# Loading the past values later in seven pairs of heads and earlier in the last

## The chip, the cores and the metric

The kernel runs on one core of a Trainium2 chip. The metric is the time of one execution in device microseconds (us); a run is the median of several executions, and one further execution is profiled. The engines are TensorE (PE), VectorE (DVE), ScalarE (ACT), GpSimd (POOL) and SyncE (SP), which here does nothing but issue transfers.

## The reference, cut to what matters

One layer of a decoder: 512 new tokens of one sequence, and one token for each of 8 sequences with a stored past of 2048 keys and values. Rows of 520 tokens are multiplied with one input projection, and the part that the change touches is the attention of the 8 single tokens over their past.

```
h = rms_norm(x);  u, gp, q, k, v, ga = split(h @ w_in)        # 2048 -> 6 x 1024, 16 heads of 64
for each of the 8 sequences and each head:                    # the sampled tokens
    positions = last 128 one by one, last 512 every 4th, last 2048 every 16th, and the token itself
    s = q . k[positions] - slope * distance;  p = softmax(s) per pattern, patterns combined
    a = sum(p * v[positions])
x = x + concat(pool_branch * silu(gp), a * silu(ga)) @ w_out;  y = rms_norm(x)
```

## The kernel before

The work is written out by hand. A **pair** is two of the 16 heads with 128 of the pool channels; there are 8 pairs (`pr` 0 to 7). A pair has 18 **chunks** (`j` 0 to 17): six column tiles of the projection, each in three chunks of 5 or 6 blocks of 128 rows. All five engines walk through the same list of steps, one chunk a step, each in its own order of instructions, and meet only at semaphores. After the 144 chunks of the input projection come 48 of the output projection. A pair's later work (`j` 18 to 25) is done in the first steps of the next pair.

A chunk of weights goes this way: SP loads it into one of three slots of `w_raw` (L442, 320 or 384 KB, three steps ahead of its use), ACT makes the rounded high part `w_hi` (L864), DVE the remainder `w_lo` (L1217), and PE multiplies (L660). SP may issue chunk n+3 only when DVE has finished chunk n, so SP runs about two steps ahead of PE. The scores, probabilities and transposes of the prompt's attention stand between a chunk's matmuls in PE's own order: in the last pair `turn_p(7, 0, 1)` (transposes, L704, in step 11) needs the normalised probabilities from ACT (L916, which needs DVE's reciprocal L1302), and `turn_p(7, 0, 2)` in step 12 also needs DVE's `p_lo(7, 0, 1)` (L1308).

The past of the 8 sequences comes in three loads of keys (`load_keys`, in steps 5, 6 and 7) and three of values (`load_values`, L469), of 512, 384 and 384 KB, all from SP's queue. The token's own row of q, k and v is spread over partitions by four small transfers each (`spread_rows`, L481, in steps 6, 8 and 12). Once the k row has landed, POOL writes it out (`send_k_row`, L1160, 4 KB), and the third part of DVE's `keys` (L1332), which multiplies in place, waits for that write:

```
def keys(pr, t):
    ...
    dve.wait_ge(k_in, 48 * pr + 48)
    dve.wait_ge(row_in[0], 16 * SQS * (pr + 1))
    if t == 2:
        dve.wait_ge(row_in[1], 16 * SQS * (pr + 1))
        dve.wait_ge(kn_st, 16 * pr + 16)
```

The steps in which DVE does `keys` and `values` are in the plan: `kq=(17, 18, 19)` and `vm=(20, 21, 21)` for the first seven pairs (USUAL), `kq=(8, 9, 10)` and `vm=(13, 14, 14)` for the last (FINAL). `values` waits for all three loads of values and for the exponentials.

Of the kernel before, what the change touches and what calls it, by code (L numbers as in the profile page):

```python
# [62 lines left out]


class Plan:
    def __init__(self, qk, s, kn, ur, kq, ex, ns, pt, vm, vr, av, pick, mix, gate):
        self.qk, self.s, self.kn, self.ur = qk, s, kn, ur
        self.kq, self.ns, self.pt, self.vm, self.vr, self.av = kq, ns, pt, vm, vr, av
        self.ex = ex
        self.pick, self.mix, self.gate = pick, mix, gate  # L70


USUAL = Plan(qk=(7, 12), s=(8, 13), kn=13, ur=15, kq=(17, 18, 19), ex=20, ns=20, pt=22,
             vm=(20, 21, 21), vr=(22, 23), av=24, pick=25, mix=(19, 21), gate=20)
FINAL = Plan(qk=(7, 11), s=(8, 12), kn=20, ur=19, kq=(8, 9, 10), ex=12, ns=17, pt=19,
             vm=(13, 14, 14), vr=(18, 20), av=20, pick=21, mix=(17, 18), gate=19)
PLANS = (USUAL,) * (PAIRS - 1) + (FINAL,)

# [42 lines left out]
def layer_step(nc, x_prompt, x_sample, state_pool, cache_k, cache_v, norm_g, w_in, pool_w,  # L121
               pool_scale, w_out, final_g, consts, y_prompt, y_sample, pool_state_p, k_win_p,
               v_win_p, pool_state_s, k_new, v_new):
    with ExitStack() as ctx:
# [110 lines left out]
        av = take(P)  # L235
# [128 lines left out]
        def due(step):  # L364

            pr, j = divmod(step, NCH)
            if pr > PAIRS:
                return ()
            late = ((pr - 1, j + NCH, PLANS[pr - 1]),) if pr > 0 else ()
            return late + (((pr, j, PLANS[pr]),) if pr < PAIRS else ())  # L370

        def chunk_of(n):

            if n < IN_CHUNKS:
                return divmod(n % NCH, 3)
            return OUT_SEQ[n - IN_CHUNKS]
# [55 lines left out]
        def _(sp):  # L432

            def load_chunk(n):
                t, c = chunk_of(n)
                lo, hi = span_of(n)
                dst = w_raw[:, n % SLOTS, 0:hi - lo, :]
                if n >= SLOTS:
                    sp.wait_ge(w_lo_done, n - 2)
                if n < IN_CHUNKS:  # L440
                    at = COL_OF[t] + P * (n // NCH)
                    sp.dma_start(dst, wi[:, lo:hi, at:at + P]).then_inc(raw_in[n % SLOTS], 16)  # L442
                    return
                cols = slice(P * t, P * t + P)
                if n >= TAIL and c > 0:
                    for at, k, m in (((0, 8, 5), (5, 6, 1)), ((0, 7, 1), (1, 13, 3)))[c - 1]:
                        sp.dma_start(dst[:, at:at + m, :],
                                     wo[:, k:k + m, cols]).then_inc(raw_in[n % SLOTS], 16)
                elif c == 2:
                    sp.dma_start(dst[:, 0:2, :], wo[:, 6:8, cols]).then_inc(raw_in[n % SLOTS], 16)  # L450
                    sp.dma_start(dst[:, 2:5, :], wo[:, 13:16, cols]).then_inc(raw_in[n % SLOTS], 16)
                else:
                    at = OUT_K[lo]
                    sp.dma_start(dst, wo[:, at:at + hi - lo, cols]).then_inc(raw_in[n % SLOTS], 16)
# [10 lines left out]
            def load_past(dst, rows, pr, t, done):  # L465

                lo = POS_AT[t][0]
                to = dst[:, P * lo:P * (lo + POS_T[t])].rearrange("p (s x) -> p s x", x=P)
                sp.dma_start(to, rows[t][:, :, P * pr:P * pr + P]).then_inc(done, 16)  # L469

            def spread_rows(pr, i):

                new_pos = slice(P * (POS - 1), P * POS)
                to = (q_rep, kk[:, new_pos], vv[:, new_pos])[i]
                sp.wait_ge(row_turned[i], pr + 1)
                if pr > 0 and i < 2:
                    sp.wait_ge(kq_sum, 3 * pr)
                elif pr > 0:
                    sp.wait_ge(av_done, pr)
                for a in range(SQS):  # L480
                    sp.dma_start(to[:, SQ * a:SQ * a + SQ],  # L481
                                 row_sq[i][SQ * a:SQ * a + NB, :].unsqueeze(1).to_broadcast(
                                     [NB, PARTS, SQ])).then_inc(row_in[i], 16)

            def load_keys(pr, t):
                if t == 0 and pr > 0:
                    sp.wait_ge(kq_sum, 3 * pr)
                load_past(kk, k_rows, pr, t, k_in)

            def load_values(pr, t):  # L490
                if t == 0 and pr > 0:
                    sp.wait_ge(av_done, pr)
                load_past(vv, v_rows, pr, t, v_in)

            def reload(i):
                k = OUT_K[i]
                r = RELOADED.index(i)
                if r == 0:
                    sp.wait_ge(pmix_st, 16 * len(RELOADED))
                    sp.wait_ge(kq_sum, 3 * PAIRS)  # L500
                sp.dma_start(mix_in[r], mix_dram[k]).then_inc(mix_back[r], 16)
# [18 lines left out]
            for step in range(IN_CHUNKS + OUT_CHUNKS):  # L520
                if step + 3 < IN_CHUNKS + OUT_CHUNKS:
                    load_chunk(step + 3)
                for pr, j, p in due(step):
                    if j == 8:
                        sp.dma_start(st_nat[0:NB * HIST, :],
                                     st[:, P * pr:P * pr + P]).then_inc(st_in, 16)
                    if j == 0:
                        if pr % 2 == 1:
                            sp.dma_start(pw_raw, pw[pr // 2:pr // 2 + 1].rearrange(
                                "a p c d -> (a p) c d")).then_inc(pw_in, 16)  # L530
                    if j in (5, 6, 7):
                        load_keys(pr, j - 5)
                    if j in (10, 11, 12):
                        load_values(pr, j - 10)
                    if j in (6, 8, 12):
                        spread_rows(pr, (6, 8, 12).index(j))
                    if j == 14:
                        sp.wait_ge(v_nat_c, pr + 1)
                        sp.dma_start(v_out[:, :, P * pr:P * pr + P],
                                     v_nat.rearrange("p (t x) -> p t x", t=QT)).then_inc(kv_st, 16)  # L540
                    if j == p.kn + 3:
                        sp.wait_ge(k_turned, pr + 1)
                        for a in range(SQS):
                            at = P * pr + SQ * a
                            sp.dma_start(k_sq_out[:, :, at:at + SQ],
                                         k_sq[SQ * a:SQ * a + SQ, :].rearrange(
                                             "p (c x) -> p c x", x=SQ)).then_inc(kv_st, 16)
                n = step - IN_CHUNKS
                if n == -4:
                    for r in range(3):  # L550
                        reload(RELOADED[r])
                for i in {-1: (3, 4, 5), 0: (6, 7, 8), 1: (9, 10), 2: (13, 14)}.get(n, ()):
                    load_split(i)
                if n == 7:
                    sp.wait_ge(m_split, len(SPLIT_ORDER))
                    sp.wait_ge(kv_st, KV_ST * PAIRS)
                    for e in range(3):
                        load_res(e)
                if n >= 0:
                    d, c = chunk_of(step)  # L560
                    if c == 0 and d >= 4:
                        sp.wait_ge(y_scaled, d - 3)
                        load_res(d - 1)
# [290 lines left out]
        def _(act):  # L854
# [82 lines left out]
            def early(pr, j, p):  # L937
# [9 lines left out]
                if j == p.qk[0]:  # L947
                    qk_hi(pr, 0)
                if j == p.qk[1] and p is USUAL:
                    qk_hi(pr, 1)  # L950
# [25 lines left out]
            def late(pr, j, p):  # L976
# [20 lines left out]
                if s1 + 1 <= j < s1 + 4:  # L997
                    exps(pr, 1, j - s1 - 1)
                if j == p.qk[1] and p is FINAL:
                    qk_hi(pr, 1)  # L1000
# [197 lines left out]
        def _(dve):  # L1198
# [289 lines left out]
            def early(pr, j, p):  # L1488
                n = NCH * pr
                s0, s1 = p.s  # L1490
                if s0 + 2 <= j < s0 + 5 and not (p is FINAL and j == p.qk[1] + 1):
                    turn_den(pr, 0, j - s0 - 2)
# [12 lines left out]
                if j == 12:  # L1505
                    if p is FINAL:
                        p_lo(pr, 0, j - s0 - 3)
# [16 lines left out]
                if j == p.pick:  # L1524
                    pick_heads(pr)
                if s0 + 3 <= j < s0 + 6 and not (p is FINAL and j == 12):
                    p_lo(pr, 0, j - s0 - 3)
# [4 lines left out]
                if s1 + 1 <= j < s1 + 4:  # L1532
                    bias_unit(pr, 1, j - s1 - 1)
                if j == 17 and p is FINAL:
                    split_pooled(pr)
# [293 lines left out]
```

## Time and profile before

| | |
|---|---|
| median of 3 runs | 850.28 us (850.09 to 852.3) |
| the profiled execution | 850.75 us, of it 848.9 from the first to the last instruction (the span) |
| PE busy | 838.7 us, 99% of the span, 6895 instructions |
| DVE busy | 555.2 us, 65% |
| ACT busy | 383.0 us, 45% |
| transfers issued by SP and others on queue 1 | 115.44 MB, 50.5% of 16 engines' span |

The profiled execution is longer than its span by 1.85 us, which lie outside of the instructions. A busy PE says that matmuls are under way, not that they run at their peak; whether an engine is waited for is read from the waits and the chain.

### The profile page before, as it was taken

To read this page: it belongs to the slowest core of one execution; us is meant where nothing else is said; L and a number is where in the kernel's file an instruction comes from. 1 tells how busy PE (TensorE), PEld (TensorE's weight loads), DVE (VectorE), ACT (ScalarE), POOL (GpSimd) and SP (SyncE) were. 2 spreads that over 40 slices of the span, in tenths; PEclk is the share of its full clock that TensorE was granted. 3 is DMA by queue.
4 is the path that set the end of the run, shared out by engine and by line. 5 is a ranking of instruction groups with operands and counts; after the bars stand their busy time and mean duration, and the time that the engine had idled before them with its cause. 6 is when DMAs were issued, how large, how long until landed. Compare 5 with 4: busy or idle time off the path is not lost.

```text
span 848.9 us, 17355 instructions
## 1 busy us (share of the span) xinstructions
PE 838.7 (99%) x6895; PEld 833.5 (98%) x6895; DVE 555.2 (65%) x1198; ACT 383.0 (45%) x849; POOL 60.7 (7%) x116
## 2 busy tenths in 40 slices
PE   9999999999999999999999999999999999999995
PEld 8999999999999999999999999999999999999995
DVE  4647784797579577857885796679888443333445
ACT  4745435523553464245435524553464354333433
POOL 2100100201010001002000101010001000000000
PEclk9999999999999999999999999999999999999999
DMA  8576347536643763574366337634759534434435
GB/s 287 144 171 163 88 127 180 132 97 176 158 110 95 192 149 86 151 186 120 97 166 172 100 100 204 156 94 129 191 164 313 145 112 116 116 106 123 120 109 202
DMA packets 236520, 124.04 MB, mean 146 GB/s; under 512 B 38256, under 2 KB 230080, under 8 KB 236416
## 3 DMA queue, kind: packets, MB, share of 16 engines
q1 hardware_dynamic: 231832, 115.44, 50.5%
q0 software_dynamic: 4608, 7.50, 2.6%
q8 instruction: 55, 0.90, 0.5%
q14 instruction: 25, 0.20, 0.1%
HBM read 106.59 MB, written 15.20 MB: 143 GB/s over the span
## 4 chain that ended last, share of the span: by engine, by line
PE 98%; DVE 1%; ACT 1%; issue 0%; DVEq 0%
PE pj L660 83%; PE ps_t L704 3%; PE pj L686 1%; PE ps_o L748 1%; PE ps_s L719 1%; PE ps_s L717 1%; PE ps_o L746 1%; PE ps_t L765 1%; PE ps_s L765 1%; PE ps_o L660 1%; PE ps_s L660 1%; PE ps_m L704 1%; PE ps_s L601 1%; PE pj L621 0%; PE pj L697 0%; PE ps_o L612 0%
## 5 line engine op out<-in xcount | busy, mean ns | idle before, releaser
L660 PE MATMUL pj<-mov_hi,w_hi 128*128 128x260 f32 x1952 | 400.8, 287 | 0.3 <-DVE mov_lo L1238 0.3
L660 PE MATMUL pj<-mov_hi,w_lo 128*128 128x260 f32 x1952 | 393.3, 283 | 0.0
L660 PE MATMUL pj<-mov_lo,w_hi 128*128 128x260 f32 x1952 | 392.5, 283 | 0.0
L660 PEld LDWEIGHTS pj<-mov_hi,w_hi 128*128 128x128 f32 x1952 | 300.9, 189 | 1.0 <-issue 0.6
L660 PEld LDWEIGHTS pj<-mov_lo,w_hi 128*128 128x128 f32 x1952 | 301.0, 189 | 0.0
L660 PEld LDWEIGHTS pj<-mov_hi,w_lo 128*128 128x128 f32 x1952 | 301.0, 189 | 0.0
L1217 DVE TENSOR_TENSOR w_lo<-w_raw,w_hi 128x640 fp32r<-128x640 f32 (+1 forms) x187 | 161.8, 865 | 157.2 <-ACT w_hi L864 156.8
L864 ACT ACTIVATE w_hi<-w_raw 128x640 fp32r<-128x640 f32 (+1 forms) x187 | 144.5, 773 | 230.2 <-PE pj L660 213.9
L924 ACT ACTIVATE pt_hi<-ps_t 128x128 fp32r<-128x128 f32 (+1 forms) x64 | 26.3, 436 | 82.4 <-PE ps_t L704 79.5
L1308 DVE TENSOR_TENSOR pt_lo<-ps_t,pt_hi 128x128 fp32r<-128x128 f32 (+1 forms) x64 | 29.7, 485 | 45.0 <-ACT pt_hi L924 44.8
L1255 DVE SCALAR_TENSOR_TENSOR arena<-pj,rstd_bc 128x260 f32<-128x260 f32 (+2 forms) x104 | 36.9, 399 | 12.1 <-PE pj L660 10.3
L908 ACT ACTIVATE arena<-arena,stat 128x128 f32<-128x128 f32 (+1 forms) x64 | 35.8, 560 | 18.5 <-DVE stat L1294 17.9
L1294 DVE CUSTOM_DVE_ANT_0 arena<-ps_s,arena 128x128 f32<-128x128 f32 (+1 forms) x64 | 29.7, 482 | 16.9 <-PE ps_s L719 16.9
L916 ACT ACTIVATE arena<-arena,stat 128x128 f32<-128x128 f32 (+1 forms) x64 | 34.2, 558 | 12.2 <-DVE stat L1302 12.0
L1063 ACT ACTIVATE arena<-arena 128x128 f32<-128x128 f32 (+1 forms) x70 | 21.8, 311 | 28.9 <-DVE arena L1662 27.2
L704 PE MATMUL ps_t<-tab,arena 128*128 128x128 f32 x218 | 34.0, 272 | 0.0
L1368 DVE TENSOR_TENSOR arena<-arena 128x128 f32<-128x128 f32 (+3 forms) x48 | 28.8, 601 | 1.6
L704 PEld LDWEIGHTS ps_t<-tab,arena 128*128 128x128 f32 x218 | 26.2, 141 | 2.1
L1335 DVE TENSOR_REDUCE arena<-arena 128x16 f32<-128x1024 f32 (+2 forms) x24 | 26.1, 1086 | 0.8
L1332 DVE TENSOR_TENSOR arena<-arena 128x1024 f32<-128x1024 f32 (+2 forms) x24 | 26.0, 1083 | 0.0
L1359 DVE TENSOR_TENSOR arena<-arena 128x1024 f32<-128x1024 f32 (+2 forms) x24 | 25.4, 1087 | 0.2
L1176 POOL DMA_DIRECT2D out<-arena x32 | 16.3, 510 | 104.7 <-DVE arena L1607 104.7
(243 smaller groups left out, 812.4 us busy)
## 6 DMA issues: line engine op xcount, KB each, us to landing
w_raw<-in_w_in SPq DMA_DIRECT2D x96, 320.0 KB, 3.5
w_raw<-in_w_in SPq DMA_DIRECT2D x48, 384.0 KB, 3.7
arena<-in_cache_k_win SPq DMA_DIRECT2D x16, 384.0 KB
arena<-in_cache_v_win SPq DMA_DIRECT2D x16, 384.0 KB
w_raw<-in_w_out SPq DMA_DIRECT2D x16, 384.0 KB, 3.5
w_raw<-in_w_out SPq DMA_DIRECT2D x16, 320.0 KB, 3.2
arena<-in_cache_k_win SPq DMA_DIRECT2D x8, 512.0 KB
arena<-in_cache_v_win SPq DMA_DIRECT2D x8, 512.0 KB
```

The source lines that it names most:

```text
L660: mm = pe.matmul(dst[h][:, 0:HT], w, m[:, k, HT * h:HT * h + HT], start=(k == 0 and i == 0), stop=(c == 2 and k == KT - 1 and i == 2))
L704: return pe.transpose(dst, src, ident[0:n, 0:n])
L864: act.activation(w_at(n)[0][:, 0:hi - lo, :], w_raw[:, n % SLOTS, 0:hi - lo, :], ACT.Copy).then_inc(w_hi_done, 1)
L908: act.activation(pb_, pb_, ACT.Exp, scale=-1.0, bias=nmax[:, i:i + 1], accum_out=den[:, i:i + 1]).then_inc(exped, 1)
L916: a = act.activation(pb_, pb_, ACT.Copy, scale=rden[:, i:i + 1])
L924: a = act.activation(pt_hi[:, 0:i + 1, P * i:P * i + P], ps_t[:, at:at + P * (i + 1)].rearrange("p (j x) -> p j x", j=i + 1), ACT.Copy)
L1217: dve.tensor_tensor(to_lo[:, 0:hi - lo, :], w_raw[:, n % SLOTS, 0:hi - lo, :], to_hi[:, 0:hi - lo, :].bitcast(F32), ALU.subtract).then_inc ...
L1255: o = dve.scalar_tensor_tensor(out=dst, in0=pj[a][h][:, c0:c1], scalar=scale, in1=rstd_bc[:, HT * h + c0:HT * h + c1], op0=ALU.mult, op1=A ...
L1294: dve.tensor_tensor_reduce(out=pbuf[r % 2][:, at:at + n], in0=ps_s[:, at:at + n], in1=nbias[:, SEQ - n:SEQ], scale=1.0, scalar=3e38, op0=A ...
L1308: o = dve.tensor_tensor(pt_lo[blk], ps_t[:, at:at + P * (i + 1)].rearrange("p (j x) -> p j x", j=i + 1), pt_hi[blk].bitcast(F32), ALU.subt ...
L1335: dve.tensor_reduce(sc_s[:, 2 * lo:2 * hi], k.rearrange("p (x e) -> p x e", e=E), AX_X, ALU.add).then_inc(kq_sum, 1)
L1368: o = dve.tensor_tensor(out, vv[:, P * to:P * (to + n)], vv[:, P * other:P * (other + n)], ALU.add)
```

## The change

The three loads of values move. In pairs 0 to 6 they are issued in steps 14, 15 and 16 in place of 10, 11 and 12; in pair 7 in steps 8, 9 and 10 in place of 10, 11 and 12. Nothing else in the program differs; no engine but SP has another order.

```
-    def __init__(self, qk, s, kn, ur, kq, ex, ns, pt, vm, vr, av, pick, mix, gate):
+    def __init__(self, qk, s, kn, ur, kq, ex, vl, ns, pt, vm, vr, av, pick, mix, gate):
...
-        self.ex = ex
+        self.ex, self.vl = ex, vl
...
-USUAL = Plan(qk=(7, 12), s=(8, 13), kn=13, ur=15, kq=(17, 18, 19), ex=20, ns=20, pt=22,
+USUAL = Plan(qk=(7, 12), s=(8, 13), kn=13, ur=15, kq=(17, 18, 19), ex=20, vl=14, ns=20, pt=22,
...
-FINAL = Plan(qk=(7, 11), s=(8, 12), kn=20, ur=19, kq=(8, 9, 10), ex=12, ns=17, pt=19,
+FINAL = Plan(qk=(7, 11), s=(8, 12), kn=20, ur=19, kq=(8, 9, 10), ex=12, vl=8, ns=17, pt=19,
...
-                    if j in (10, 11, 12):
-                        load_values(pr, j - 10)
+                    if p.vl <= j < p.vl + 3:
+                        load_values(pr, j - p.vl)
```

SP's order in the first pair before, from chunk 12's load to the stores of the prompt's keys (`in_w_in` is a chunk of weights, `in_cache_v_win` a load of values, L481 a row being spread, L539 and L545 the stores of the prompt's values and keys):

```order
25 L442 DMA w_raw<-in_w_in 128x6x128
26 L442 DMA w_raw<-in_w_in 128x5x128
27 L469 DMA arena<-in_cache_v_win 128x8x128
28 L442 DMA w_raw<-in_w_in 128x5x128
29 L469 DMA arena<-in_cache_v_win 128x6x128
30 L442 DMA w_raw<-in_w_in 128x6x128
31 L469 DMA arena<-in_cache_v_win 128x6x128
32 L481 DMA arena<-arena 128x1x32 x4
33 L442 DMA w_raw<-in_w_in 128x5x128 x2
34 L539 DMA out<-arena 128x4x128
35 L442 DMA w_raw<-in_w_in 128x6x128
36 L442 DMA w_raw<-in_w_in 128x5x128
```

The same place with the change:

```order
25 L442 DMA w_raw<-in_w_in 128x6x128
26 L442 DMA w_raw<-in_w_in 128x5x128 x2
27 L442 DMA w_raw<-in_w_in 128x6x128
28 L481 DMA arena<-arena 128x1x32 x4
29 L442 DMA w_raw<-in_w_in 128x5x128 x2
30 L469 DMA arena<-in_cache_v_win 128x8x128
31 L539 DMA out<-arena 128x4x128
32 L442 DMA w_raw<-in_w_in 128x6x128
33 L469 DMA arena<-in_cache_v_win 128x6x128
34 L442 DMA w_raw<-in_w_in 128x5x128
35 L469 DMA arena<-in_cache_v_win 128x6x128
36 L545 DMA out<-arena 32x16x32 x4
```

The value loads have moved behind the spreading of the v row, next to the two stores, and between the last chunk of this pair and the first two of the next. The following six pairs change in the same way.

SP's order in the last pair before, from chunk 11 to the v row (the first L481 is the k row, the second the v row; `in_state_pool` is a small load of the pool's history):

```order
215 L442 DMA w_raw<-in_w_in 128x5x128
216 L525 DMA arena<-in_state_pool 120x128
217 L481 DMA arena<-arena 128x1x32 x4
218 L442 DMA w_raw<-in_w_in 128x6x128
219 L442 DMA w_raw<-in_w_in 128x5x128
220 L469 DMA arena<-in_cache_v_win 128x8x128
221 L442 DMA w_raw<-in_w_in 128x5x128
222 L469 DMA arena<-in_cache_v_win 128x6x128
223 L442 DMA w_raw<-in_w_in 128x6x128
224 L469 DMA arena<-in_cache_v_win 128x6x128
225 L481 DMA arena<-arena 128x1x32 x4
```

The same place with the change:

```order
208 L442 DMA w_raw<-in_w_in 128x5x128
209 L525 DMA arena<-in_state_pool 120x128
210 L469 DMA arena<-in_cache_v_win 128x8x128
211 L481 DMA arena<-arena 128x1x32 x4
212 L442 DMA w_raw<-in_w_in 128x6x128
213 L469 DMA arena<-in_cache_v_win 128x6x128
214 L442 DMA w_raw<-in_w_in 128x5x128
215 L469 DMA arena<-in_cache_v_win 128x6x128
216 L442 DMA w_raw<-in_w_in 128x5x128
217 L442 DMA w_raw<-in_w_in 128x6x128
218 L481 DMA arena<-arena 128x1x32 x4
```

The first and largest load of values now stands ahead of the k row's four transfers, and the second and third stand directly behind them, with chunks 12 and 13 between.

## Rows read from the trace of the kernel before

**Rows 1.** The page: span, busy time, the chain that ended last.

```profile
span 848.9 us, 17355 instructions
PE 838.7 (99%) x6895; PEld 833.5 (98%) x6895; DVE 555.2 (65%) x1198; ACT 383.0 (45%) x849; POOL 60.7 (7%) x116
PE 98%; DVE 1%; ACT 1%; issue 0%; DVEq 0%
```

**Rows 2.** The waits of PE: line, what it waited for, total, times, longest.

```profile
PE ps_s L601 <- DVE mov_lo L1222: 1.2, 1, 1.2
PE pj L660 <- DVE mov_lo L1238: 0.3, 1, 0.3
```

**Rows 3.** SP's timeline, pair 4, steps 15 to 17: start, duration, line.

```profile
391.57 3.00 SPq L442 DMA_DIRECT2D w_raw<-in_w_in  x2
...
397.58 0.51 SPq L442 DMA_DIRECT2D w_raw<-in_w_in  x1
```

**Rows 4.** L442's transfers from 100 to 620 us, issue to landing.

```profile
DMA to landing us min/median/max: 3.0/3.6/10.7
```

**Rows 5.** ACT's timeline, then DVE's, where pair 4's late loads are used.

```profile
402.05 0.85 ACT L864 ACTIVATE w_hi<-w_raw 128x768 fp32r<-128x768 f32 x1
...
421.05 1.23 DVE L1359 TENSOR_TENSOR arena<-arena 128x1024 f32<-128x1024 f32 x1
```

**Rows 6.** SP's timeline, last pair, steps 7 to 11.

```profile
593.85 1.48 SPq L469 DMA_DIRECT2D arena<-in_cache_k_win  x1
595.37 0.73 SPq L442 DMA_DIRECT2D w_raw<-in_w_in  x1
...
597.33 2.71 SPq L481 DMA_DIRECT2D arena<-arena  x4
600.08 1.40 SPq L442 DMA_DIRECT2D w_raw<-in_w_in  x2
601.53 0.64 SPq L469 DMA_DIRECT2D arena<-in_cache_v_win  x1
```

**Rows 7.** L442 in the last pair: the issues at 595.37 and at 600.08, to landing.

```profile
DMA to landing us min/median/max: 6.6/6.6/6.6
DMA to landing us min/median/max: 3.6/3.6/3.6
```

**Rows 8.** POOL's timeline, last pair: the k row is written out.

```profile
603.33 0.55 POOL L1160 DMA_DIRECT2D out<-arena  x1 [43.15 <-DMA arena<-arena]
```

**Rows 9.** L1160 to landing: all eight pairs, then the last pair alone.

```profile
DMA to landing us min/median/max: 3.2/7.3/8.8
DMA to landing us min/median/max: 7.1/7.1/7.1
```

**Rows 10.** Pair 2, timelines of SP and POOL, and that L1160 to landing.

```profile
209.33 0.64 SPq L469 DMA_DIRECT2D arena<-in_cache_v_win  x1
209.20 0.58 POOL L1160 DMA_DIRECT2D out<-arena  x1 [15.59 <-DMA arena<-arena]
DMA to landing us min/median/max: 3.2/3.2/3.2
```

**Rows 11.** DVE's timeline, last pair, steps 10 and 11.

```profile
610.60 1.08 DVE L1332 TENSOR_TENSOR arena<-arena 128x896 f32<-128x896 f32 x1
...
615.18 0.83 DVE L1217 TENSOR_TENSOR w_lo<-w_raw,w_hi 128x640 fp32r<-128x640 f32 x1 [0.83 <-ACT w_hi L864]
618.66 0.56 DVE L1308 TENSOR_TENSOR pt_lo<-ps_t,pt_hi 128x384 fp32r<-128x384 f32 x1
```

**Rows 12.** ACT's timeline, last pair, steps 10 and 11.

```profile
608.86 0.83 ACT L864 ACTIVATE w_hi<-w_raw 128x768 fp32r<-128x768 f32 x1
613.26 0.62 ACT L916 ACTIVATE arena<-arena,stat 128x384 f32<-128x384 f32 x1 [0.93 <-DVE stat L1302]
```

**Rows 13.** PE's timeline, last pair: the transposes of steps 11 and 12.

```profile
615.73 0.49 PE L704 MATMUL ps_t<-tab,arena 128*128 128x128 f32 x3
620.37 0.60 PE L704 MATMUL ps_t<-tab,arena 128*128 128x128 f32 x4
```

## Prediction

> **What bounds the kernel now.** I read the page first: PE is busy for 838.7 of 848.9 us, and the chain that ended last is PE for 98% [rows 1]. A busy share alone doesn't tell whether PE waits, so the list of PE's waits comes next: 1.2 and 0.3 us, both in the first steps, and none after that [rows 2]. The reader is to see that nothing the other engines or the transfers do costs PE time at present. So the change can give back at most 1.5 us, and that not in the places it touches; the question is whether it makes PE wait. For that I read, for each load that moves, when what is queued behind it is used.
>
> **Pairs 0 to 6, the loads in steps 14 to 16.** Two things become later. The values themselves: the third load goes out ahead of the chunk that SP now issues at 397.58 [rows 3], and DVE multiplies the values at 421.05 [rows 5], 23.5 us later. The longest landing of any chunk of weights, many of them queued behind such loads, is 10.7 us, the median 3.6 [rows 4]; the values have 13 us to spare. The chunks behind them: the next pair's first chunk is issued at 391.57 [rows 3] and rounded by ACT at 402.05 [rows 5], 10.5 us later. Even the worst landing, 10.7 us, would hold ACT for 0.2 us, and PE needs `w_lo` only after DVE's pass over it. What hides these seven moves is therefore SP's lead of some two steps; if it were gone, each pair would pay what the landing exceeds. I take 0 for them, bounds 0 and 0.2 us a pair, 1.4 us in all. The chunks that lose their neighbour in steps 10 to 12 land earlier, which is worth nothing, as PE doesn't wait for them.
>
> **Pair 7, the loads in steps 8 to 10.** Here something small is overtaken. Before, SP issues the last key load at 593.85, chunk 11 at 595.37, the k row's four transfers from 597.33, chunks 12 and 13 from 600.08, and the first values only at 601.53 [rows 6]. The k row has landed when POOL starts its write at 603.33 [rows 8], that write takes 7.1 us to land [rows 9], which is 610.4, and DVE's third `keys`, which waits for it, starts at 610.60 [rows 11]. So a wait that costs nothing today is met with 0.2 us to spare. Now step by step:
>
> 1. The first load of values, 512 KB, is put ahead of the k row in SP's queue. What a load ahead costs what comes behind it: chunk 11 with a 384 KB key load just ahead took 6.6 us to land, chunk 12 without one 3.6 [rows 7], so 3.0 us for 384 KB, and 4.0 us for 512 KB by size (an estimate from these rows; chunk 12 is itself the larger chunk, so it isn't too high). POOL starts at 607.3 in place of 603.33. The bounds are 3.0 us, if a load costs the same whatever its size, and 4.0.
> 2. POOL's write then competes with the second and third value loads, which SP issues right behind the k row, as before it competed with the first. The trace has eight such writes, 3.2 to 8.8 us, median 7.3, in the last pair 7.1 [rows 9]. The fast one of pair 2 was issued at 209.20, just ahead of a value load at 209.33 [rows 10]; that of pair 7 went out 1.8 us behind one. After the change value loads stand ahead of it in any case, so I take 7.1: landing at 614.4. The bounds are 3.2 and 8.8, which give 609.5 and 616.1.
> 3. DVE's third `keys` starts at 614.4 in place of 610.60, 3.8 us late (bounds 0 and 5.5). DVE works in order, so all that follows in its queue moves by as much. It idles for 0.83 us before the `w_lo` at 615.18, but that is for ACT's `w_hi` [rows 11], which stands in ACT's queue behind the normalisation at 613.26, which waits 0.93 us for DVE's reciprocal [rows 12]. The idle time moves along and gives nothing back.
> 4. What is late next is PE's transposes. Those of step 11 start at 615.73 [rows 13], and the normalisation that they need ends at 613.88 [rows 12]: 1.85 us to spare. Those of step 12 start at 620.37 [rows 13] and need `p_lo`, which ends at 619.22 [rows 11]: 1.15 us to spare. PE loses 3.8 - 1.85 = 1.95 us at the first and another 0.7 at the second, together 3.8 - 1.15 = 2.65 us. Behind that place PE and DVE have moved alike but for 1.15 us. The rest of the program is PE's chain, so the loss stands at the end.
>
> Chunk 12's weights stand behind the same load. They landed at 600.08 + 3.6 = 603.7 [rows 6, 7], would land at 607.7, and ACT rounds them at 608.86 [rows 12]: hidden, by 1.1 us. The v row's four transfers go out behind less than before, and `values`, in steps 13 and 14, gets its loads earlier; both are worth nothing, since PE doesn't wait.
>
> **The sum.** The profiled execution took 850.75 us, 1.85 outside its span; with 2.65 us more it would take 853.4. The median of the runs is 0.47 below that execution, so I forecast a median of 852.9 us, 0.3% slower.
>
> **Rivals.** *The k row's write slips through.* POOL issues on a queue of its own; if its few packets pass between those of the value loads instead of waiting for them, they land after 3.2 us, as in pair 2 [rows 10], at 610.5, and DVE doesn't wait. It decides for every landing up to 611.75 (610.60 and the 1.15 us to spare); the time is 850.3. Against it stand the median of 7.3 and the last pair's own 7.1 [rows 9]. The Trainium skill's page DMA: Bandwidth & Descriptors, section Queues, rings and completion order, speaks for it: an engine takes turns between the queues that it has work for, a packet of at most 64 descriptors at a time, so that by this rule the write would wait for one turn and not for a whole load. By that rule the sum would be 0 and the time 850.3; pair 2's 3.2 us agrees with it, the median and pair 7's own row don't. I give it 0.27.
>
> *The weights are starved too.* If the 512 KB cost over 5.1 us ahead of chunk 12, in place of 4.0, its `w_hi` at 608.86 is late, and it stands in ACT's queue ahead of all that PE's transposes need; and if landings in the other pairs exceed 10.5 us, each pays up to 0.2 us. That would come on top of a late k row at its bound: 4.35 + 1.4 and about 1 us for chunk 12, up to 857. For it speaks that SP's issues take longer behind a full queue (1.48 us at 593.85 against 0.64 at 601.53 [rows 6]); against it that the longest landing in 119 is 10.7 [rows 4]. I give it 0.10.
>
> *Faster.* It would need PE to have lost time to the collisions that are taken away. The list of waits leaves 1.5 us in the first steps [rows 2], so that even all of it, 848.8, would be less than what a measurement here can tell. I give 0.03 to a gain by something that the waits don't show.
>
> **How the numbers follow.** The late k row has 0.60. Its time goes from 850.3, at a landing of 611.75, to 854.7 (616.1: 5.5 - 1.15 = 4.35 us); half of the eight writes take 7.3 us or more, so its own likely range is 851.5 to 854.7. About 0.3% (2.55 us, so 852.83) is what a measurement of this kernel can tell from no change. The forecast lies at that bound; with a write of over 7.0 us the loss is above it, and more than half were [rows 9]: I put 0.33 of the 0.60 above it and 0.27 below, as step 1 is an estimate. With the starved weights that makes slower 0.43; with the write that slips through same 0.54; faster 0.03. The range goes from the rival without a loss, 850.0 with the spread of the runs, to the bound of the late row, 854.8; outside are the starved weights and the gain, and some of the edges.
>
> **What the changed kernel's profile would show.** Right: POOL's L1160 in the last pair starts near 607.3 and lands near 614.4; DVE waits before the third L1332, named as a wait for that transfer; PE shows two waits in steps 11 and 12 of the last pair, for ACT's L916 and DVE's L1308, of about 2.0 and 0.7 us; pairs 0 to 6 take the same time as before, and their writes of the k row land in some 3.5 us, because no value load is near. Step 1 is wrong if POOL starts within a microsecond of 603.3, step 2 if the write lands in about 3 us, step 4 if DVE waits and PE doesn't. The whole would be wrong if PE waited in pairs 0 to 6, above all at the first chunks of the next pair.

## The result and the profile after

The changed kernel takes 853.9 us (median of 17 runs, 850.83 to 856.12), the kernel before 850.33 us (median of 17, 849.51 to 852.3). The ratio is 1.0041, with a 95% interval of 1.0032 to 1.0049: slower by 0.4%, some 3.5 us. The profiled execution took 853.5 us. Here and below the ratio is not simply the quotient of the two medians. One of the 84 runs of the kernel before that were measured beside the experiments took 1167.12 us at a mean granted clock of 0.656, a slow state, and is in no ratio.

The page of the changed kernel, to be read beside [rows 1]: the instructions are the same in number, the span is longer by 2.7 us, and the chain that ended last now runs through DMA, DVE and SP's queue as well.

```profile
span 851.6 us, 17355 instructions
PE 836.7 (98%) x6895; PEld 830.4 (98%) x6895; DVE 555.3 (65%) x1198; ACT 382.8 (45%) x849; POOL 60.8 (7%) x116
PE 93%; DMA 2%; DVE 2%; SPq 1%; ACT 1%; issue 0%; DVEq 0%; ACTq 0%
```

PE's waits after (columns as in [rows 2]):

```profile
PE ps_t L704 <- ACT arena L916: 2.8, 1, 2.8
PE ps_s L621 <- DMA arena<-in_x_prompt: 1.4, 1, 1.4
PE ps_s L601 <- DVE mov_lo L1222: 1.2, 1, 1.2
PE ps_t L704 <- DVE pt_lo L1308: 0.6, 1, 0.6
PE pj L660 <- DVE w_lo L1245: 0.6, 1, 0.6
```

Two of them lie in the last pair and are new, both before transposes of L704, 2.8 and 0.6 us. The other three lie in the first 15 us, where executions differ whatever is done to the value loads, the first of which goes out long after. Between 16 and 600 us PE is never idle, and runs as many matmuls as before. Windows of before, then of after (length, busy time and instructions of PE, PEld, DVE, ACT and POOL, granted clock, share of the transfers, GB/s):

```profile
16.00:600.00 584.00, 584.00 (x4814) 580.57 (x4813) 424.01 (x916) 268.51 (x539) 52.11 (x97) 1.00 0.54 140
```

```profile
16.00:600.00 584.00, 584.00 (x4814) 580.57 (x4813) 423.48 (x914) 267.62 (x538) 51.44 (x96) 1.00 0.54 141
```

So pairs 0 to 6 cost nothing, and the loss is in the last pair. Its chain from SP to PE, one view of the changed kernel for each engine. SP's timeline (start, duration, line), beside [rows 6]:

```profile
594.48 0.64 SPq L469 DMA_DIRECT2D arena<-in_cache_k_win  x1
595.16 1.11 SPq L442 DMA_DIRECT2D w_raw<-in_w_in  x1
...
597.54 0.63 SPq L469 DMA_DIRECT2D arena<-in_cache_v_win  x1
598.28 5.23 SPq L481 DMA_DIRECT2D arena<-arena  x4
603.55 0.47 SPq L442 DMA_DIRECT2D w_raw<-in_w_in  x1
604.06 1.45 SPq L469 DMA_DIRECT2D arena<-in_cache_v_win  x1
```

POOL's write of the k row, and its issue to landing (beside [rows 8, 9]): first the last pair, then all eight.

```profile
607.98 0.56 POOL L1160 DMA_DIRECT2D out<-arena  x1 [48.69 <-DMA arena<-arena]
DMA to landing us min/median/max: 6.4/6.4/6.4
DMA to landing us min/median/max: 1.6/2.9/6.4
```

DVE's timeline (beside [rows 11]; the bracket is the idle time before an instruction and what ended it):

```profile
609.91 0.96 DVE L1217 TENSOR_TENSOR w_lo<-w_raw,w_hi 128x768 fp32r<-128x768 f32 x1 [2.06 <-ACT w_hi L864]
614.48 1.09 DVE L1332 TENSOR_TENSOR arena<-arena 128x896 f32<-128x896 f32 x1 [3.60 <-DMA out<-arena]
...
622.54 0.56 DVE L1308 TENSOR_TENSOR pt_lo<-ps_t,pt_hi 128x384 fp32r<-128x384 f32 x1
```

ACT's timeline (beside [rows 12]):

```profile
609.04 0.85 ACT L864 ACTIVATE w_hi<-w_raw 128x768 fp32r<-128x768 f32 x1 [0.88 <-DMA w_raw<-in_w_in]
...
617.14 0.62 ACT L916 ACTIVATE arena<-arena,stat 128x384 f32<-128x384 f32 x1 [5.69 <-DVE stat L1302]
```

PE's timeline (beside [rows 13]):

```profile
617.81 0.55 PE L704 MATMUL ps_t<-tab,arena 128*128 128x128 f32 x3 [2.81 <-ACT arena L916]
...
623.25 0.63 PE L704 MATMUL ps_t<-tab,arena 128*128 128x128 f32 x4 [0.59 <-DVE pt_lo L1308]
```

The reader is to see one delay handed on five times: the k row's four issues take 5.23 us behind the value load, POOL's write starts at 607.98, it lands after 6.4 us, DVE's third `keys` waits 3.60 us for it, ACT's normalisation waits for DVE, and PE for both.

One thing must be known before times of the two traces are set side by side. In its first 15 us the changed kernel's profiled execution got ahead, and the lead was still there in the last pair, ahead of the loss: 0.88 us on PE (the first score matmul of step 10, L717, starts at 609.91 against 610.79) and 0.78 us on DVE (the second `keys` starts at 605.23 against 606.01). Below, "on the program's own clock" adds this back: PE's transposes of step 11 come 617.81 + 0.88 - 615.73 = 2.96 us late, those of step 12 623.25 + 0.88 - 620.37 = 3.76 us. That lead is why the two profiled executions are only 2.75 us apart.

### The profile page after: what moved, and what is told of

The parts are those of the page before. It is cut to its first block, busy times and chain, and to the rows that moved or that the text cites. A ratio compares the mean times of both kernels' runs of the same rounds, so it can differ in the third digit from the quotient of the medians.

```text
span 851.6 us, 17355 instructions
## 1 busy us (share of the span) xinstructions
PE 836.7 (98%) x6895; PEld 830.4 (98%) x6895; DVE 555.3 (65%) x1198; ACT 382.8 (45%) x849; POOL 60.8 (7%) x116
## 4 chain that ended last, share of the span: by engine, by line
PE 93%; DMA 2%; DVE 2%; SPq 1%; ACT 1%; issue 0%; DVEq 0%; ACTq 0%
PE pj L660 80%; PE ps_t L704 3%; PE pj L686 1%; PE ps_o L748 1%; PE ps_s L719 1%; DMA arena<-in_x_prompt 1%; PE ps_s L717 1%; PE ps_o L746 1%; DMA out<-arena 1%; PE ps_s L765 1%; PE ps_t L765 1%; PE ps_o L660 1%; PE ps_s L660 1%; PE ps_m L704 1%; DMA arena<-arena 1%; SPq L481 1%
## 5 line engine op out<-in xcount | busy, mean ns | idle before, releaser
L704 PE MATMUL ps_t<-tab,arena 128*128 128x128 f32 x218 | 34.1, 273 | 3.4 <-ACT arena L916 2.8
L704 PEld LDWEIGHTS ps_t<-tab,arena 128*128 128x128 f32 x218 | 26.1, 141 | 5.9 <-ACT arena L916 3.8
```

The source lines that it names most:

```text
L704: return pe.transpose(dst, src, ident[0:n, 0:n])
```

## The experiments

The theory: the whole loss is the last pair's, and it is the k row's write, late and then slow behind value loads, that holds DVE's third `keys`. The rivals are that the moved loads of pairs 0 to 6 cost something, that chunk 12's weights behind the 512 KB do it, and that the value loads only take bandwidth from everything. All edits are to the changed kernel.

### Each half of the change alone

`e1_usual_only` keeps the new places in pairs 0 to 6 and gives the last pair its old ones:

```
-FINAL = Plan(qk=(7, 11), s=(8, 12), kn=20, ur=19, kq=(8, 9, 10), ex=12, vl=8, ns=17, pt=19,
+FINAL = Plan(qk=(7, 11), s=(8, 12), kn=20, ur=19, kq=(8, 9, 10), ex=12, vl=10, ns=17, pt=19,
```

> Only pairs 0 to 6 load their values later (steps 14 to 16); the last pair is as before (10 to 12). Theory (the whole loss is the late write of the k row in the last pair): no wait of PE after the first steps, ratio to before 1.000, 850.3 us; the write of the k row in the last pair lands some 7 us after its issue, as before. Rival (part of the loss is the seven moves, whose value loads hold up the next pair's weights): slower than before by what the last pair's two waits of 2.8 and 0.6 us leave of the 3.6 us, and by more if those waits are overcome elsewhere: 850.5 to 852.

Measured: 850.61 us beside 850.61 for the kernel before, ratio 1.0004 (0.9993 to 1.0014). The time alone lies in the rival's range as well; what decides is that PE waits in the first 15 us only (1.4, 1.2 and 0.5 us).

`e2_final_only` does the reverse:

```
-USUAL = Plan(qk=(7, 12), s=(8, 13), kn=13, ur=15, kq=(17, 18, 19), ex=20, vl=14, ns=20, pt=22,
+USUAL = Plan(qk=(7, 12), s=(8, 13), kn=13, ur=15, kq=(17, 18, 19), ex=20, vl=10, ns=20, pt=22,
```

> Only the last pair loads its values earlier (steps 8 to 10); pairs 0 to 6 are as before (10 to 12). Theory: the same loss as the whole change, 853.5 to 854.0 us, ratio 1.004; DVE waits some 3.6 us for the write of the k row, PE 2.8 and 0.6 us at the transposes of steps 11 and 12. Rival (the seven moves cost or give something): a time outside 853 to 855.

Measured: 853.82 beside 850.61, ratio 1.0033 (1.0022 to 1.0045). PE's waits in its profiled execution, POOL's write, and DVE's third `keys`:

```profile
PE ps_t L704 <- ACT arena L916: 0.9, 1, 0.9
PE ps_t L704 <- DVE pt_lo L1308: 0.6, 1, 0.6
```

```profile
606.57 0.56 POOL L1160 DMA_DIRECT2D out<-arena  x1 [46.48 <-DMA arena<-arena]
DMA to landing us min/median/max: 6.6/6.6/6.6
```

```profile
613.31 1.09 DVE L1332 TENSOR_TENSOR arena<-arena 128x896 f32<-128x896 f32 x1 [2.72 <-DMA out<-arena]
```

The seven pairs are free, within the 0.14% that e1's interval leaves, and the last pair costs the rest. The same chain is there, and shorter: this profiled execution took 852.51 us, less than the median of its kernel, and POOL began in it 3.3 us later than before on the program's own clock (DVE's lead is 0.09 us here), where in the changed kernel's it is 5.4.

### The k row ahead of the value load

`e3_row_first` swaps the two blocks in SP's step, in all pairs, so that step 8's value load goes out behind the k row:

```
-                    if p.vl <= j < p.vl + 3:
-                        load_values(pr, j - p.vl)
                     if j in (6, 8, 12):
                         spread_rows(pr, (6, 8, 12).index(j))
+                    if p.vl <= j < p.vl + 3:
+                        load_values(pr, j - p.vl)
```

> The whole change, but in step 8 of the last pair SP issues the four transfers of the k row ahead of the first load of values in place of behind it; the value loads stay in steps 8, 9 and 10. Theory as forecast (the row standing behind the 512 KB is what is late, by 4 to 5.5 us, and the write then takes its usual 7 us): POOL starts its write near 602 to 603, it lands near 609.5 to 610.5, DVE waits under 1 us, PE not at all: 850.3 us. Rival (three value loads close behind the write are enough by themselves): the write takes over 9 us, DVE waits 2 us or more, PE over 1 us: 851.5 to 853.5.

Measured: 854.01 beside 850.61, ratio 1.0033 (1.0019 to 1.0046). The expectation missed: as slow as the changed kernel, though the k row was in time. POOL started at 603.43, and its write landed after 7.0 us, 610.4. The chunk that now stands directly behind the 512 KB is chunk 12 (SP's issue at 601.78); its issue to landing, then ACT, which waited for it, and PE:

```profile
DMA to landing us min/median/max: 11.2/11.2/11.2
```

```profile
612.98 0.85 ACT L864 ACTIVATE w_hi<-w_raw 128x768 fp32r<-128x768 f32 x1 [4.14 <-DMA w_raw<-in_w_in]
```

```profile
618.07 0.88 PE L704 MATMUL ps_t<-tab,arena 128*128 128x128 f32 x3 [3.08 <-ACT arena L916]
```

PE waits 3.08 us at the same transposes, for another reason: the late `w_hi` stands in ACT's queue ahead of the normalisation. Here the prediction's rival of the starved weights is at work. So the step has two things that are due by about 610, the k row and chunk 12, and in these runs whichever stands right behind the load pays.

`e10_row_first_stores_late` asks whether POOL's two 260 KB stores, issued right behind the k row's write, make chunk 12 so slow. It is e3 with the last pair's two stores moved behind the v row's write:

```
-                if pr > 0:
+                if 0 < pr < PAIRS - 1:
                     send_split(pr - 1 + PAIRS)
                 send_v_row(pr)
+                if pr == PAIRS - 1:
+                    send_split(pr - 1 + PAIRS)
```

> As the run in which the k row goes ahead of the first value load, but POOL issues its two large stores of the last pair (260 KB each) behind the write of the v row, some 17 us later. Theory formed on that run (chunk 12's weights, which stood directly behind the 512 KB, took 11.2 us because those stores ran beside it): chunk 12 lands in 6 to 8 us, near 609, ACT waits for it under 1 us, PE not at all after the first steps: 850.3 to 850.9 us. Rival (standing behind the load is enough, with or without the stores): it still takes 10 us or more, PE waits some 3 us, 853 to 854 us.

Measured: 851.18 beside 850.42, ratio 1.0013 (1.0004 to 1.0021). Chunk 12's landing and ACT's `w_hi`:

```profile
DMA to landing us min/median/max: 9.6/9.6/9.6
```

```profile
610.90 0.84 ACT L864 ACTIVATE w_hi<-w_raw 128x768 fp32r<-128x768 f32 x1 [2.37 <-DMA w_raw<-in_w_in]
```

The landing lies between the two expectations, and so does the time. Without the stores 1.6 us of the 11.2 are gone, and with them most of PE's wait (0.5 and 0.6 us are left); the larger part of the landing stays. The trace of `e4_final9`, the last experiment below, shows whose it is: there chunk 12 goes out ahead of the load and lands at 603.7, when the stores have only just been issued (603.15), and chunk 13 goes out directly behind the load. Their issues to landing:

```profile
DMA to landing us min/median/max: 3.6/3.6/3.6
DMA to landing us min/median/max: 11.9/11.9/11.9
```

So the place behind the load, without the stores, makes 9.6 us of 3.6, and the stores add 1.6, each from a single execution.

### A k row write that DVE needn't wait for

`e5_own_write` lets POOL write the k row from the tile in which it was turned, `row_sq[1]`, before it is spread; DVE's `keys` then has no write to wait for, and the next pair's turning waits for it instead. SP's order is the changed kernel's:

```
-                pool.wait_ge(row_in[1], 16 * SQS * (pr + 1))
-                pool.dma_start(kn_out[:, P * pr:P * pr + P], kk[0:P:PARTS, new_pos]).then_inc(kn_st, 16)
+                pool.wait_ge(row_turned[1], pr + 1)
+                for a in range(SQS):
+                    lo, at = SQ * a, P * pr + SQ * a
+                    pool.dma_start(kn_out[:, at:at + SQ],
+                                   row_sq[1][lo:lo + NB, :]).then_inc(kn_st, 16)
...
-                    dve.wait_ge(kn_st, 16 * pr + 16)
...
+                    if i == 1:
+                        dve.wait_ge(kn_st, 16 * SQS * pr)
```

> The whole change, but POOL writes the new k row out from the small tile that SP also spreads it from, as four transfers with rows of 128 B, once DVE has turned it; DVE's third keys no longer waits for that write, only for the spread row. Theory (the write is what holds DVE): DVE's third keys waits for the spread row alone, under 0.5 us, PE doesn't wait after the first steps: 850.3 us, ratio 1.000. Rival (the weights of chunk 12, which ACT waited 0.9 us for, or the spread row itself are enough): PE keeps waits of 1 us or more at the transposes of the last pair, 851.3 to 853.5.

Measured: 850.92 beside 850.61, ratio 1.0003 (0.9992 to 1.0014); PE waits nowhere in the last pair. But POOL, freed of its wait for the spread row, also issued its two stores at 600.27 in place of 608.5, out of the way of all that is late. `e9_own_write_gated` puts that wait back ahead of the stores alone:

```
                 send_k_row(pr)
+                pool.wait_ge(row_in[1], 16 * SQS * (pr + 1))
                 if pr > 0:
```

> As the run with the write of the k row from its own small tile, but POOL waits for the spread k row before it issues the two large stores that follow (260 KB each), as it does in the changed kernel; in the earlier run these went out some 8 us sooner. Theory (only the write of the k row holds DVE): DVE's third keys has no wait for a transfer of over 0.5 us, PE no wait after the first steps, ratio 1.000, 850.3 to 850.9 us. Rival (it was the stores' earlier issue that took the loss away, by leaving the weights alone): ACT waits for chunk 12's weights and PE at the transposes, 852 to 854 us.

Measured: 850.32 beside 850.42, ratio 1.0 (0.9991 to 1.0009). POOL's stores and DVE's third `keys`:

```profile
608.25 0.56 POOL L1171 DMA_DIRECT2D hi_scratch<-stg_hi  x1 [12.99 <-DMA arena<-arena]
```

```profile
609.54 0.96 DVE L1221 TENSOR_TENSOR w_lo<-w_raw,w_hi 128x768 fp32r<-128x768 f32 x1 [1.15 <-ACT w_hi L864]
610.41 1.08 DVE L1335 TENSOR_TENSOR arena<-arena 128x896 f32<-128x896 f32 x1
```

The spread row lands late (POOL is released at 608.25), the stores go out late, the loads stand where the change puts them, and nothing is lost: `keys` follows `w_lo` without a wait. It is the wait for the write that costs the changed kernel its time; here the late row by itself, the transfers' competition and chunk 12 cost nothing as long as nobody waits for the write.

### How large the load ahead is

`e6_small_first` loads the last pair's values in the order 384, 512, 384 KB:

```
-                if t == 0 and pr > 0:
+                if t == (1 if pr == PAIRS - 1 else 0) and pr > 0:
                     sp.wait_ge(av_done, pr)
...
-                        load_values(pr, j - p.vl)
+                        load_values(pr, j - p.vl if p is USUAL else (1, 0, 2)[j - p.vl])
```

> The whole change, but in the last pair the order of the value loads is 384, 512, 384 KB, so that 384 KB and not 512 KB stand ahead of the k row. Theory (the row is late in proportion to what stands ahead of it, by 5.5 us for 512 KB as measured): it comes 1.4 us sooner than in the changed kernel, POOL starts near 606.6, DVE waits some 2.2 us, PE some 2 us in all: 852.2 to 852.8 us. Rival (what holds the row is the queue being full, whatever the load): no difference from the whole change, 853.5 to 854.

Measured: 852.42 beside 850.42, ratio 1.0027 (1.0016 to 1.0038). POOL starts at 606.97, which with DVE's lead of 0.35 us in this execution is 4.0 us later than before, where the changed kernel's was 5.4 us later. The write takes 6.4 us again, the k row's issues are shorter, and so are PE's waits:

```profile
598.89 4.44 SPq L481 DMA_DIRECT2D arena<-arena  x4
```

```profile
PE ps_t L704 <- ACT arena L916: 1.6, 1, 1.6
...
PE ps_t L704 <- DVE pt_lo L1308: 0.6, 1, 0.6
```

Three quarters of the load, and a smaller loss, of the size expected. That the lateness goes by the load's size is borne out by SP's issues of the k row, which took 5.18 to 5.73 us behind 512 KB (the changed kernel, e2, e5, e7, e9, e11), 4.44 behind 384 KB, and 2.55 to 3.58 with no value load ahead (before, e1, e3, e4, e10). The row's landing, which releases POOL, scatters more: 5.2 to 5.7 us late behind 512 KB in the changed kernel, e7, e9 and e11, but 3.3 in e2, less than the 4.0 here.

### What makes the write itself slow

`e7_two_later` puts the second and third load of the last pair into steps 11 and 12, to take them away from the write:

```
-                    if p.vl <= j < p.vl + 3:
+                    if p is USUAL and p.vl <= j < p.vl + 3:
                         load_values(pr, j - p.vl)
+                    if p is FINAL and j in (8, 11, 12):
+                        load_values(pr, (8, 11, 12).index(j))
```

> The whole change, but in the last pair only the first load of values is issued in step 8; the second and third in steps 11 and 12. The k row still stands behind 512 KB, but no value load follows close behind it. Theory (the row's lateness, some 5 us, and the write's 6 to 7 us beside the following loads are both needed): POOL starts its write near 607 to 608, it lands in 3 to 3.5 us, near 611, DVE waits 0.5 to 1.5 us, PE under 0.5: 850.3 to 850.9 us. Rival (the row's lateness alone is enough): the write still takes 5 us or more, DVE waits over 2 us, PE 1 to 3.5 us: 851.5 to 854.

Measured: 854.46 beside 850.42, ratio 1.0048 (1.0033 to 1.0064). It missed, because the edit didn't do what it was for: the second load was issued at 608.07, still ahead of the write at 609.83, which took 7.2 us and held DVE for 5.1.

```profile
608.07 0.77 SPq L469 DMA_DIRECT2D arena<-in_cache_v_win  x1
```

```profile
609.83 0.55 POOL L1162 DMA_DIRECT2D out<-arena  x1 [48.87 <-DMA arena<-arena]
DMA to landing us min/median/max: 7.2/7.2/7.2
```

`e11_two_at_12` puts both into step 12:

```
+                    if p is FINAL and j == 8:
+                        load_values(pr, 0)
+                    if p is FINAL and j == 12:
+                        for t in (1, 2):
+                            load_values(pr, t)
```

> The whole change, but in the last pair the second and third load of values go out together in step 12, behind POOL's write; in the run with steps 11 and 12 one of them was still issued 1.8 us ahead of that write. The k row stands behind 512 KB as in the changed kernel. Theory (the write takes 6 to 7 us only where a value load stands ahead of it): it lands in 3 to 4 us, near 611.5, DVE waits 0.5 to 1.5 us, PE under 0.7: 850.3 to 851.2 us. Rival (the chunks of weights behind the 512 KB, or POOL's own stores, slow it as much): it takes 5 us or more, PE waits 1.5 us or more, 852 to 855 us.

Measured: 850.95 beside 850.46, ratio 1.0006 (0.9996 to 1.0016). SP issues them at 611.25, behind POOL's write at 608.55, and chunks of weights from 603.85 on:

```profile
603.85 7.36 SPq L442 DMA_DIRECT2D w_raw<-in_w_in  x4
611.25 2.54 SPq L469 DMA_DIRECT2D arena<-in_cache_v_win  x2
```

```profile
608.55 0.56 POOL L1165 DMA_DIRECT2D out<-arena  x1 [49.45 <-DMA arena<-arena]
DMA to landing us min/median/max: 3.8/3.8/3.8
```

```profile
612.52 1.09 DVE L1337 TENSOR_TENSOR arena<-arena 128x896 f32<-128x896 f32 x1 [1.71 <-DMA out<-arena]
```

With the same stores right behind it, and chunks of weights but no value load directly ahead, the write takes 3.8 us in place of 6.4, and DVE's wait falls from 3.60 to 1.71 us; the k row itself is as late as in the changed kernel, which leaves PE 1.1 and 0.6 us in this execution, more than expected. So it is the value loads that slow the write, and chunks of 320 and 384 KB do not: in pairs 0 to 6 of the changed kernel, too, only chunks stand directly ahead of it, and it lands in 1.6 to 3.5 us. Two of the three value loads have the same 384 KB as a chunk; why they differ no run shows.

### One step later

`e4_final9` gives the last pair steps 9 to 11, so that the first load stands behind the k row, with chunk 12 in between:

```
-FINAL = Plan(qk=(7, 11), s=(8, 12), kn=20, ur=19, kq=(8, 9, 10), ex=12, vl=8, ns=17, pt=19,
+FINAL = Plan(qk=(7, 11), s=(8, 12), kn=20, ur=19, kq=(8, 9, 10), ex=12, vl=9, ns=17, pt=19,
```

> The whole change, but the last pair's value loads go out in steps 9, 10 and 11, so that the k row and chunk 12's weights stand ahead of the first of them. Theory (what is lost is lost by whatever stands behind the 512 KB and is needed soon: the k row in the changed kernel, chunk 12 with the row put first): both are ahead now, POOL starts its write near 602 to 603, it lands by 610.5, ACT waits for chunk 12 under 0.5 us; chunk 13 lands near 612, in time; PE doesn't wait after the first steps: 850.3 to 850.9 us. Rival (any value load near step 8 costs time, as the engines of the transfers are busy then): PE waits 1 us or more in the last pair, 851.5 us or more.

Measured: 850.07 beside 850.46, ratio 0.9996 (0.9985 to 1.0006). POOL starts at 602.60, its write takes 8.1 us, and DVE waits a little:

```profile
610.87 1.09 DVE L1332 TENSOR_TENSOR arena<-arena 128x896 f32<-128x896 f32 x1 [1.11 <-DMA out<-arena]
```

PE doesn't wait in the last pair: 1.11 us is within what the prediction found to spare. No version measured beats the kernel before; PE's waits there, 1.5 us [rows 2], are all that another order of these loads could give back.

## Why the prediction came out as it did

The forecast was 852.9 us, and the time is 853.9. Mechanism, place and sign were right, and the loss was under-sized by about 1 us: step 1 by 1.4 us, of which step 2, taken 0.7 us too long, gave half back. That the two errors are of opposite sign is luck.

**Pairs 0 to 6 at nothing: right.** PE is never idle from 16 to 600 us, and e1, which has these moves alone, measures no difference beyond its interval. The writes of the k row there became faster, a median of 2.9 us over all eight in place of 7.3, and that is worth nothing, as predicted.

**Step 1, POOL 4.0 us later: mis-sized.** POOL started at 607.98, where 607.3 was forecast, but with DVE's lead of 0.78 added it is 5.4 us late, beyond the bound of 4.0. Set beside [rows 6, 8] the 5.4 come apart: SP begins the k row's issues 1.7 us later (598.28 + 0.78 - 597.33), they take 5.23 us in place of 2.71, 2.5 more, and from the end of the issues to POOL's start it is 4.5 us (607.98 - 603.51) in place of 3.3, 1.2 more. The step had costed the load by what a chunk of weights lost in landing behind one [rows 7]; that SP is held in its issues too was seen, but used only for a rival. That the cost goes by the load's size was right for the issues (4.44 us behind 384 KB, 5.18 to 5.73 behind 512); the whole lateness varies between executions, as e2's 3.3 us behind 512 KB beside e6's 4.0 behind 384 shows.

**Step 2, a write of 7.1 us: right in kind, 6.4 measured.** The rival that it slips through is refuted for this kernel: with a value load ahead the last pair's write took 6.4 to 8.1 us in nine traces (before, after, e1, e2, e3, e4, e6, e7, e10), with none directly ahead 3.8 (e11). By the Trainium skill's page DMA: Bandwidth & Descriptors, section Queues, rings and completion order, as the prediction read it, the write would have waited for one turn and not for a whole load. The trace disagrees with that reading; whether the engines took turns no run shows. Nor was pair 2's 3.2 us [rows 10] a case of slipping through. The prediction noted that it went out just ahead of a value load but kept it as the rival's example; pair 4 of the kernel before, the other short one, went out just ahead as well (views as in [rows 10]):

```profile
367.49 0.64 SPq L469 DMA_DIRECT2D arena<-in_cache_v_win  x1
367.25 0.57 POOL L1160 DMA_DIRECT2D out<-arena  x1 [10.98 <-DMA arena<-arena]
DMA to landing us min/median/max: 3.4/3.4/3.4
```

Of the 16 writes of the kernel before and of e2, the four issued ahead of the first value load or within 0.2 us behind it landed in 3.1 to 3.4 us, the twelve issued some 0.6 us or more behind it in 5.6 to 8.8. So the row that spoke for the rival was one of a write ahead of the load, and the changed kernel's is behind.

**Step 3, DVE 3.8 us late and nothing given back: right, and mis-sized by steps 1 and 2.** The third `keys` began at 614.48, on the program's own clock 4.66 us late (614.48 + 0.78 - 610.60). The idle 0.83 us before the next `w_lo` moved along unchanged, as forecast. e5 and e9, where DVE doesn't wait for the write, show that this wait is the cause.

**Step 4, PE loses 1.95 and 0.7 us: the spare was right, the sum 3.76 for 2.65.** A DVE that is 4.66 us late, less the 1.85 and 1.15 to spare, gives 2.81 and 3.51; the transposes came 2.96 and 3.76 late. What is left over at the second, 0.25 us, is 0.15 between the end of `p_lo` (623.10) and the transposes (623.25), a handover that the step counted as nothing, and the 0.10 by which the leads of PE and DVE differ.

**Chunk 12 hidden by 1.1 us: not hidden, but without a cost.** It landed at 603.55 + 5.5 = 609.05, where 607.7 was forecast, and ACT waited 0.88 us for it. DVE was about to wait longer for the write, so nothing came of it here; e9, where the write's wait is gone, loses nothing either. In e3 it is this chunk that sets the end.

**The size of the whole.** Of the 17 runs, nine have a mean granted clock of 0.995 or less and a median of 854.58 us; the other eight have 853.13. The sum's 852.9, which has no term for the clock, lies beside the latter. The first 15 us move single executions as well: the last eight matmuls of L601 there start at 8.25 us before and in e9, at 6.73 in e1, by nothing that the edits touch. So a single execution tests the sum to about a microsecond only. None of the 83 runs of the kernel before that are kept beside the experiments is at 0.995 or less.

## What to carry to other kernels

Where a chain on one engine holds all the time, list for each transfer that will be overtaken what is queued behind it and how much its consumer has to spare: here an engine that was busy for 65% met a 4 KB write with 0.2 us in hand, and that decided the change. Here a small transfer queued behind a large one paid in the issues of its queue, 2.5 to 3.0 us behind 512 KB, and in most executions in landing too, and with the row put ahead what took its place paid, so that a move must be costed for every neighbour. Before a fast case in the trace is taken as a sign that a collision is harmless, look whether it was in the collision at all: both short writes had gone out ahead of the load. A wait that protects a tile from being overwritten can be removed by writing from another copy; that made the new order free here, and the order then gave nothing back, because PE had waited for nothing.

## What the runs showed of the hardware that was not expected

The granted clock of PE fell after its longer waits. Windows of e3 (behind 3.08 us of waiting), of e7 (behind 3.82 us), and of the changed kernel (behind 2.81 us), columns as above:

```profile
618.00:621.00 3.00, 2.93 (x14) 2.93 (x15) 1.72 (x5) 2.98 (x8) 0.00 (x0) 0.52 0.80 180
```

```profile
621.00:625.00 4.00, 4.00 (x20) 4.00 (x19) 2.78 (x5) 3.93 (x9) 0.56 (x1) 0.50 0.38 95
```

```profile
618.00:621.00 3.00, 3.00 (x27) 3.00 (x27) 1.72 (x5) 2.95 (x8) 0.00 (x0) 1.00 0.46 102
```

With 0.52 on average, nearly all of it at the lower level of 1.2 GHz (0.50), PE ran 14 matmuls in 3 us, at 1.00, 2.4 GHz, 27; at the faster pace the 13 missing are worth some 1.4 us (an estimate from these two windows). So a wait can cost more than its own length; e7's profiled execution, at 857.79 us, is the longest of all changed versions. This goes with the counts of runs at a mean clock of 0.995 or less: nine of 12 of e7, nine of 17 of the changed kernel, seven of 12 of e2 and five of 8 of e3, but none of the 44 of e4, e9, e10 and e11, where no wait of PE in the last pair of the profiled execution is over 1.1 us. The order isn't strict: e2's profiled waits are 0.9 and 0.6 us, e1 and e5, without such a wait, have three such runs of 24, and e6 has two of 8. That the fall of the clock makes up the rest of the loss in those runs is argued from this, not shown: only profiled executions tell where the clock fell, and in the changed kernel's it did not.
